# The wait ahead of a load into a ring place: the low part of the slab that lay there in place of its products

## The reference

```
x  = first_block(x, c, ctx, ...)      # depth 1
       ada:   m = silu(c) @ w_ada + b_ada
       mixer: u = modulate(x) @ w_in;  y = mix(u) @ w_out
       conv_ffn: a = dwconv2d_grid(h @ w_up);  (gelu(gate) * val) @ w_down
x  = second_block(x, c_2, ctx_2, ...) # depth 2
       layer 0: ab_mixer (products with ab_w_in, ab_w_out), then mlp
       layer 1: c_mixer  (products with c_w_in, c_w_out), then mlp
       mlp: square(relu(h @ w1)) @ w2,   w1 1024 x 4096, w2 4096 x 1024
       each layer: mod = silu(c) @ ada_w[layer] + ada_b[layer]
```

## Time and profile before

| | us |
|---|---|
| median of 3 runs | 2866.36 |
| lowest and highest run | 2865.56, 2872.26 |
| profiled execution, its own time | 2861.79 |
| span of the profiled execution | 2860.0 |
| TensorE busy in it | 2467.1 |
| GpSimd busy | 1021.7 |
| mean granted clock, share of full | 0.927 |

### The profile page before, as it was taken

The page is one execution under the profiler, slowest core; times in us unless marked ns, Lnnn a source line. Parts: engine busy times, 40 slices in busy tenths (PEclk is TensorE's granted clock), DMA queues, the critical chain, the costliest instruction groups (busy, mean ns, idle before and its releaser), DMA issues. The chain is left out here.

```text
span 2860.0 us, 35805 instructions
## 1 busy us (share of the span) xinstructions
PE 2467.1 (86%) x14567; PEld 1990.7 (70%) x14567; DVE 1232.7 (43%) x1959; ACT 806.9 (28%) x1358; POOL 1021.7 (36%) x627
## 2 busy tenths in 40 slices
PE   4877758899999799695778899999988787899998
PEld 3655636678777589483566788888876566678887
DVE  1530752775544500676644414141516645233322
ACT  1312323333332522232513112121215244222222
POOL 1421623455555423031034424342525001455554
PEclk8888868899999799886998999999999899999999
DMA  7235011244443112000001523232321000123231
GB/s 243 72 110 173 1 53 60 94 147 147 146 144 118 51 55 73 31 1 8 1 30 60 162 98 103 81 102 76 114 72 58 32 1 1 59 89 103 88 103 59
DMA packets 222828, 230.00 MB, mean 80 GB/s; under 512 B 7131, under 2 KB 218799, under 8 KB 222671
## 3 DMA queue, kind: packets, MB, share of 16 engines
q1 hardware_dynamic: 222671, 227.76, 24.7%
HBM read 225.65 MB, written 2.10 MB: 80 GB/s over the span
## 5 line engine op out<-in xcount | busy, mean ns | idle before, releaser
L1064 POOL TENSOR_TENSOR w_lo<-ring,w_hi 128x1024 fp32r<-128x1024 f32 x128 | 306.8, 2398 | 446.0 <-ACT w_hi L1059 446.0
L1059 ACT ACTIVATE w_hi<-ring 128x1024 fp32r<-128x1024 f32 x128 | 135.9, 1063 | 751.3 <-PE ps L1123 690.5
L1777 DVE SCALAR_TENSOR_TENSOR xT<-ps,mods,xT 128x512 f32<-128x512 f32 (+1 forms) x160 | 108.2, 683 | 527.5 <-PE ps L1123 475.0
L1121 PE MATMUL ps<-hidden_hi,w_hi 128*128 128x512 f32 (+1 forms) x768 | 274.9, 358 | 5.3 <-POOL hidden_lo L2125 4.9
L2045 DVE SCALAR_TENSOR_TENSOR ffn_sums<-ps,cols,ffn_sums 128x441 f32<-128x441 f32 (+2 forms) x352 | 214.8, 687 | 137.6 <-ACT ffn_sums L1968 137.6
L1122 PE MATMUL ps<-hidden_lo,w_hi 128*128 128x512 f32 (+1 forms) x768 | 272.7, 355 | 0.0
L1123 PE MATMUL ps<-hidden_hi,w_lo 128*128 128x512 f32 (+1 forms) x768 | 272.4, 355 | 0.0
L1121 PE MATMUL ps<-h_hi,w_hi 128*128 128x512 f32 (+1 forms) x720 | 258.0, 358 | 5.9 <-POOL w_lo L1064 4.4
L1122 PE MATMUL ps<-h_lo,w_hi 128*128 128x512 f32 (+1 forms) x720 | 255.7, 355 | 0.0
L1123 PE MATMUL ps<-h_hi,w_lo 128*128 128x512 f32 (+1 forms) x720 | 255.2, 355 | 0.0
L777 POOL TENSOR_TENSOR ring_low<-ring,w_halves 128x1024 fp32r<-128x1024 f32 x50 | 120.6, 2423 | 357.8 <-ACT w_halves L773 357.8
(11 more groups left out here) (437 smaller groups left out, 5273.1 us busy)
## 6 DMA issues: line engine op xcount, KB each, us to landing
ring<-in_mlp_w SPq DMA_DIRECT2D x64, 1024.0 KB, 5.3
ring<-in_ada_w SPq DMA_DIRECT2D x48, 1024.0 KB, 6.8
ring<-in_w_ada SPq DMA_DIRECT2D x24, 1024.0 KB, 7.8
ring<-in_ffn_w_up SPq DMA_DIRECT2D x22, 1024.0 KB, 5.2
ring<-in_ab_w_in SPq DMA_DIRECT2D x11, 1024.0 KB, 5.2
ring<-in_ffn_w_down SPq DMA_DIRECT2D x12, 768.0 KB, 6.1
ring<-in_w_in SPq DMA_DIRECT2D x8, 1024.0 KB, 9.9
ring<-in_c_w_in SPq DMA_DIRECT2D x6, 1024.0 KB, 5.0
```

What stands on the lines that cost most here:

```text
L1059: act.activation(w_hi[m][:, 0:x["kt"], :], ring[:, x["n"] % NS, 0:x["kt"], m * P:(m + 1) * P], ACT.Copy).then_inc(SW["w_hi"].sem, 1)
L1064: pool.tensor_tensor(w_lo[m][:, 0:x["kt"], :], ring[:, x["n"] % NS, 0:x["kt"], m * P:(m + 1) * P], w_hi[m][:, 0:x["kt"], :].bitcast(F32), ...
L1121: pe.matmul(o, w_hi[m][:, k, :], h, start=(k == 0), stop=False)
L1777: return nc.vector.scalar_tensor_tensor(x, bank, column_of(gates, t * 2 + 2 * gate + r), x, ALU.mult, ALU.add)
```

## The change

`split_off` is a table from a slab number to a pair of semaphore and value. Every slab whose halves are split into `w_hi` and `w_lo` tiles has an entry: in `split_stage` all slabs of the kind "w" (not ada slabs), in the feed-forward stage all up and down slabs (the entry is made by the unit with m = 1, the second half). The value is the count of `w_lo` at which GpSimd has made both low parts of that slab. In `load_slabs` the load of slab n waits for that pair if slab n - 4 has an entry, and for `mm_done` as before if it has none, so behind an ada slab and in the units stages. `turns_alike` no longer forms loops in a stretch that holds such a slab. The other engines' programs are the same.

```diff
--- before.py
+++ after.py
@@ -280,6 +280,7 @@
             add_slabs("mlp_w1_2", 1, whole, cols_of(1024 * q, 4), 2)
             add_slabs("mlp_w2_2", 1, [(1024 * q, KT)], cols_of(0, 4), 2)
         issued = [0]
+        split_off = {}
 
         def slab_source(entry, i=None, d_row=0, d_col=0):
 
@@ -303,13 +304,16 @@
                 if n >= NS:
 
                     used = signals[n - NS + 1]
-                    sp.wait_ge(mm_done, used if i is None else i * per_turn + used)
+                    if n - NS in split_off:
+                        sp.wait_ge(*split_off[n - NS])
+                    else:
+                        sp.wait_ge(mm_done, used if i is None else i * per_turn + used)
                 sp.dma_start(ring[:, n % NS, 0:stream[n][3], :], slab_source(stream[n], i, *step))\
                   .then_inc(slot_loaded[n % NS], 16)
 
             def turns_alike(n, period):
 
-                if n < NS or n + 2 * period > upto:
+                if n < NS or n + 2 * period > upto or any(x - NS in split_off for x in range(n, upto)):
                     return 1, None, 0
                 steps = [(stream[n + period + s][2] - stream[n + s][2], stream[n + period + s][4] - stream[n + s][4])
                          for s in range(period)]
@@ -1019,6 +1023,13 @@
                     history = history + [(k, v + seg["kinds"][k] * (reps - 1)) for k, v in history[-n_u:]]
                     prev_w = dict(prev_w, n=prev_w["n"] + seg["ns"] * (reps - 1))
                 segs.append(seg)
+            w_no = 0
+            for items, reps in segments:
+                for t in range(reps):
+                    for it in items:
+                        if it[0] == "w":
+                            split_off[it[1] + t * len(items)] = (SW["w_lo"].sem, SW["w_lo"].at(2 * w_no + 2))
+                            w_no += 1
             done[0] = max(until, segments[0][0][0][1] + sum(len(items) * reps for items, reps in segments))
 
             def run(eng, body):
@@ -1882,6 +1893,7 @@
 
         sig = lambda ins, n: ins.then_inc(R[n].sem, 1)
         wait = lambda eng, n, v: eng.wait_ge(R[n].sem, R[n].at(v))
+        split_off.update({u[1]: (SW["w_lo"].sem, SW["w_lo"].at(i + 1)) for u, i in index_of.items() if u[2] == 1})
         with nc.Block() as block:
             @block.sync
             def _(sp):
```

## The result

The changed kernel takes 2836.86 us (median of 6 runs, 2833.87 to 2839.27) against 2867.12 us of the kernel before on the same chip (6 runs, 2865.21 to 2877.02). The ratio is 0.9882, with a 95% interval of 0.9868 to 0.9896: faster by 1.2%, or 30.3 us between the medians. The profiled execution took 2839.27 us, at a mean clock of 0.923.

What follows compares the result with a forecast made beforehand. TensorE's work was taken to set the time, so earlier loads return only its idling and low clock: 16.3 + 1.7 + 6.6 + 3.5 = 28.1 us, from 2866.36 to 2838.3 us, range 2832 to 2850.

Steps and rivals of the forecast that it cites:

- Which places: Gains only in the feed-forward stage and the first MLP; nothing in the other split stages.
- Feed-forward, idle: Feed-forward stage: ScalarE's slab waits end, 16.3 of TensorE's 17.3 us idling gained, 1.0 left for waits not followed singly.
- 1.7 the clock: End of the feed-forward stage: 1.7 us gained from the low clock around the longest wait (0 to 1.8).
- The chain: Feed-forward stage: U load issued one period earlier, second behind A; period in U and A 12.64 us, TensorE the bound.
- First MLP: 6.6 of idling and 3.5 of clock: Earlier first `w2` load: 6.6 us of TensorE idling gained, 0.6 left, plus 3.5 us from the low clock behind it.
- The term of 0: Stage openings: six loads now run beside the engines there and slow them by 0 us.
- The written-out loops: SP's two register loops in the split stages, now written out: 0 us.
- VectorE's chain stays: Rival, feed-forward stage: TensorE still waits for taps, 9.1 us stay, 2847.4 us; chance 0.10.
- MLP only: Rival: the feed-forward stage gives nothing, only the first MLP's 10.1 us come, 2856.3 us; chance 0.05.
- the new wait never decides: Rival: the A load ahead in SP's queue holds until the old moment, no gain, 2866.4 us; chance 0.05.
- The clock: Rival, feed-forward stage: banks without pauses lower the clock to 1.2 GHz, up to 2926.8 us; chance 0.02.

Runs made afterwards that it cites:

- e9: Kernel before with its old waits, ScalarE's relus put ahead of the slab copies in all split stages: 2866.65 us, ratio 0.9995.
- e10: Kernel before, old waits; only the first `w2` slab's copies in the first MLP put behind all three `ada_rows` copies: 2864.92 us, ratio 0.9989.
- e5: Kernel before, old waits; in the feed-forward stage centre tap and `ada_rows` copy put ahead of the next slab's copy: 2849.98 us, ratio 0.9918.
- e2: Changed kernel, but only the load of the first MLP's first `w2` slab waits for a low part: 2857.88 us, ratio 0.9949.
- e3: Changed kernel, loops still written out, but every load waits for products as before: 2871.94 us, ratio 1.001.

## Why the prediction was right

*Which places.* It named two places and held the rest for nothing. The stages agree: 20.9 and 9.1 us there, 0.2 and 1.2 us in the input stage and the last MLP. The 1.2 us are no gain of the change: with the old waits the last MLP took 359.5 us (e9) to 361.0. Part of the closeness of the sum is luck: the first stage gave 2.9 us more than forecast and the second 1.0 us less.

*Feed-forward, idle: 16.3 of 17.3.* This is the term that was a little mis-sized. All 17.3 us went; the 1.0 held back for waits that could not be followed was not needed, since TensorE has no idle row between 520 and 920. The stage gained 20.9 us and not 18.0. Of that, 17.3 are idle time and 1.7 the clock. The first 16 us of the stage cost 0.6 more than before, at a clock of 0.80 where it was 0.84 (0.04 x 2 x 16 = 1.3 us more at 1.2 GHz, half of it lost). What is left is 20.9 + 0.6 - 17.3 - 1.7 = 2.5 us. The sequence of products is the same in both traces, so the two can be laid side by side, and 2.2 of the 2.5 us lie at the ten A slabs whose small products waited for `ada_rows`. One such place, first in the kernel before, then in the changed one:

```profile
590.33 0.39 PE L1937 MATMUL ps<-ffn_h_hi,ffn_w_lo 128*128 128x512 f32 x1
591.52 0.61 PE L626 MATMUL ps<-mats,ada_rows 128*128 128x2 f32 x4 [0.80 <-ACT ada_rows L635]
591.98 0.48 PE L1935 MATMUL ps<-ffn_h_hi,ffn_w_hi 128*128 128x512 f32 x1
```

```profile
587.23 0.40 PE L1949 MATMUL ps<-ffn_h_hi,ffn_w_lo 128*128 128x512 f32 x1
587.46 0.50 PE L630 MATMUL ps<-mats,ada_rows 128*128 128x2 f32 x4
587.82 0.48 PE L1947 MATMUL ps<-ffn_h_hi,ffn_w_hi 128*128 128x512 f32 x1
```

From the last product ahead to the small ones it is 1.19 us where it is 0.23 without a wait: 0.96 us lost, of which the view shows 0.80, because it counts the product ahead for 0.39 us. From the small ones to the next product it is 0.46 where it is 0.36. So a wait at this place costs about a quarter of a microsecond more than the idle time shown. A wait for taps does not: the period of the earlier trace rows holds one pause, 1.25 us, and 13.89 - 1.25 = 12.64 us, against 12.65 measured.

```profile
543.74 0.47 PE L1935 MATMUL ps<-ffn_h_hi,ffn_w_hi 128*128 128x512 f32 x1 [1.25 <-DVE ffn_sums L2045]
```

The 1.7 us of the clock were there in this pair of profiles, but not in every execution: in e10, with the same order and waits in this stage, the same pause (2.42 us at 883.36) had a clock of 1.00 from 862 to 892.

*The chain.* Period 12.64 predicted, 12.65 measured. The U load is issued as second of a pair behind A, a period ahead, as the prediction derived from SP's order and not from the diff. The A load still waits for products, and this costs nothing. VectorE's chain was priced with 1.0 us of margin and had at least 2.0. The taps end at 554.50, 11.6 us behind the start of the A products, as the prediction has it, but TensorE asks for the bank only behind the next A products, at 556.55. The prediction took the end of the U for that moment and left out its own 1.03 us for A, so it held this rival for nearer than it was. TensorE never waits for the taps.

*First MLP: 6.6 of idling and 3.5 of clock.* The pause left was 0.41 us (0.6 predicted), so 6.8 gained, and the clock behind it is 1.00. Together 10.3 against 10.1. The stage gained 9.1, because its first 20 us ran at 0.89 where it was 0.92 (1.2 us more at 1.2 GHz, 0.6 lost); 0.3 us are in a later pause, 1.81 us long at 1833.72 where it was 1.47; the last 0.3 us I can't place. The load went out at 1598.83. Forecast was 2.4 us behind the start of the low part (1607.52 in the old trace); measured are 2.43 us behind 1596.40. The slab landed by 1607.48, 8.7 us behind its issue, where the prediction had about 12; this margin was larger than forecast and changed nothing.

*The other claims.* ScalarE's waits for slabs left the feed-forward stage, where it was claimed. In the first MLP one of 9.8 us stayed. It ended at 1607.48 and cost TensorE nothing: the 0.41 us before 1617.18 come from the copy of the second half at 1614.95, which products released, and from the relus behind it, as the prediction has it. The openings got their transfers, and the engines there did not slow down. The 32 us ahead of the feed-forward stage, of the kernel after and then of the one before:

```profile
484.00:516.00 32.00, 20.22 (x219) 9.37 (x217) 19.89 (x32) 19.03 (x31) 5.16 (x3) 0.57 0.10 34
```

```profile
484.00:516.00 32.00, 21.22 (x220) 10.37 (x219) 20.13 (x32) 19.18 (x31) 4.73 (x3) 0.57 0.01 1
```

VectorE needs 19.89 us for its 32 instructions with a DMA share of 0.10, and 20.13 with 0.01; the taps in the stage take 9.73 us as before. The term of 0 stands. The Trainium skill, "SBUF — State Buffer", section "Who interferes with whom", says that DMA never contends with a compute engine, and these rows agree. The written-out loops cost nothing (1.001, 0.9997 to 1.0024).

*The rivals.* "VectorE's chain stays" falls with the waits after: no row of TensorE on `ffn_sums`. "MLP only" and "the new wait never decides" fall with the stage's 20.9 us. "The clock" falls with 1.00 from 520 to 920: 400 us of banks without a pause held 2.4 GHz. What the prediction did not see is that only in the first MLP the load was late by itself; in the feed-forward stage its lateness cost time only through ScalarE's order. It read the chain load, copy, `centre`, taps and priced the load; e5 shows that the same chain could be cut one step later.

## What to carry to other kernels

When an engine that nobody suspects waits for ScalarE, look at what ScalarE itself waited for just before, and at what lay ready behind it in its program: moving that ahead of the wait can give all of the gain without an earlier load (21 us here, and 42 in a stage that the change leaves alone). Then ask the other question, whether the slab would be on time if its copy were the last thing in line; if the wait only changes its releaser, as in the first MLP, the load must start earlier, and here one load of 64 was enough. A relaxed wait in an in-order queue helps only as far as its neighbour lets it, so name the neighbour's wait in the estimate.

## What the runs showed of the hardware that was not expected

The stretch from the feed-forward stage to the first MLP holds the same 3335 products in every kernel here. It took from 607.1 to 615.6 us in thirteen profiles, at clocks of 0.88 to 0.86, without a tie to any edit. This is as large as the gain in the first MLP, so a difference of two profiled spans can mislead by several microseconds. The length of a stage, from its first product to its last, is better in two of the stages: with the old order and waits the feed-forward stage took 424.2 to 425.5 us and the first MLP 588.4 to 590.1. The input stage is not as steady: unchanged, it took 182.8 to 187.8 us.

The two long pauses had a low clock behind them (2.38 us of standing: 3.6 us at 1.2 GHz in 862 to 892; 7.17 us: 10.1 us in 1631 to 1642), while nineteen shorter ones of up to 1.25 us in the feed-forward stage had none, and neither had one of 1.81 us in the changed first MLP (1.00 from 1820 to 1850). A pause of the same kind does not always do the same: at the place of the 2.38 us, pauses of 2.07 (e2), 2.19 (e3) and 2.50 us (e9) had a clock of 0.94 in the 30 us around them, and that of 2.42 us in e10 had 1.00. The Trainium skill, "TensorE: Matmul & The Clock Gate", section "A second HAM failure mode: psum-queue depth-cycling", reports a lowered clock from repeated brief pauses; neither trace of this case shows it, with pauses (1.00 from 528 to 940) or without.
